# First up projection of a macaron layer: pairs 13 to 21 by seven block products, with the modulation dots moved around them

## The chip, the cores and the metric

The kernel runs on one core of one Trainium2 chip. The metric is the device time of one execution in microseconds (us), median of three runs.

## What is computed

One encoder layer of width 1024 on 512 tokens, in float32: LayerNorm, a half-step SwiGLU FFN, a mixing sub-layer (latent attention beside causal pooling), a second half-step FFN. The change is in the first FFN:

```python
c_act = jax.nn.silu(c)
mod = (c_act @ w_ada[l] + b_ada[l]).reshape(B, N_SUBLAYERS, 3, D)
shift, scale, gate = mod[:, :, 0], mod[:, :, 1], mod[:, :, 2]
h = x * (1.0 + scale[:, 0, None, :]) + shift[:, 0, None, :]
g, u = jnp.split(h @ ffn1_w_in[l], 2, axis=-1)     # 1024 x 5632
y = (jax.nn.silu(g) * u) @ ffn1_w_out[l]           # 2816 x 1024
x = _layernorm(ALPHA * x + 0.5 * gate[:, 0, None, :] * y, post_ln_g[l, 0], post_ln_b[l, 0])
```

## The kernel before

The core's five engines run programs of their own, written out in order by hand, and wait for one another through semaphores. Features lie on the 128 partitions, the 512 tokens along the free dimension. To keep float32 accuracy each operand is split in a high part (rounded to fp32r on ScalarE) and a low part (the rest, on VectorE or GpSimd), and each product is three matmuls: high by high, high by low, low by high.

Weights come in units of 128x1024 (512 KB), that is eight 128x128 blocks, one output tile each. SP loads unit n into a ring of three (`raw`), ScalarE makes w_hi (`act_hi`), VectorE w_lo (`dve_lo`), four slots deep and three units ahead. Pair t of the first up projection (F1) is unit 2t (gate) and 2t+1 (up): 48 matmuls of 512 columns. Then ScalarE applies Silu to the gate bank, VectorE multiplies with the up bank, ScalarE and GpSimd split the result into a_hi, a_lo. There are 22 pairs. The down projection takes three units for each of eight output tiles m (the third with six blocks only), 24 units, and ends each tile by a residual on VectorE. In tile 1 TensorE runs one matmul over x tile 0 (`shift_mean`, which wants ScalarE's rounding of that tile), VectorE copies the result (`shift`), and GpSimd subtracts it from all eight x tiles.

In the second FFN pairs 5 to 21 are already made otherwise (`block_products`). The 2x2 scheme of seven products takes the two halves of the contraction and the two halves of the tokens against combinations of the gate and up blocks: products p1 to p7, each 4 x 3 matmuls of 256 columns, 84 in all. Three of the weight combinations are made by adding DMAs from GpSimd's queue and by VectorE (`weight_sums`), four combinations of h (T) once by VectorE (`combine_h`), the partial results pass through ScalarE's copies (p_copy, u_copy). The SP queue loads for each pair: c, d (raw_d), a3 and ab. The x tiles give up their space for it and are spilled to HBM ahead and reloaded at the start of the down projection.

The 72 modulation columns (`mod`) are dots: VectorE multiplies a tile of w_ada (128x1024, 512 KB, loaded by SP) by c_act and sums it. Sixteen are done at the start. The other 56 come through `ada_ring`, two slots, one after each w_lo of the first up projection (38) and one a unit in the down projection (18). `derive_in`, `derive_gb` and `derive_gate` are small VectorE steps on their results, and `rope_chunk` are VectorE steps for the rotary angles.

## Time and profile before

| what | value |
|---|---|
| median of 3 runs | 938.01 us (937.66 to 938.11) |
| profiled execution, its own time | 938.53 us |
| its span, first to last instruction | 936.7 us |
| TensorE busy | 924.4 us |
| VectorE busy | 600.4 us |
| ScalarE busy | 422.3 us |
| GpSimd busy | 276.1 us |

The span is what the trace covers; the time of the execution is 1.8 us more. An engine that is busy all the time sets the length of the stretch, and an idle one costs nothing unless that engine waits for it. Matmuls overlap, so a matmul's cost is the distance from one start to the next, not its own duration.

### The profile page before, as it was taken

How to read it: one execution, taken by the hardware profiler on the slowest of the kernel's cores; microseconds unless marked ns; L12 is line 12 of the kernel's file. 1: busy time of each engine (PE TensorE's matmuls, PEld its weight loads, DVE VectorE, ACT ScalarE, POOL GpSimd, SP SyncE). 2: the span in 40 equal slices, each digit the busy share in tenths (PEclk: the TensorE clock that was granted, in tenths of full speed). 3: DMA queues.
4: the chain of work that ended last, by engine and by line, in shares of the span. 5: the costliest groups of instructions: out<-in, count | busy, mean ns of one | idle time of the engine just before them, and what ended most of it. 6: DMA issues, size and time to landing. Idle time of an engine off the chain costs nothing.

```text
span 936.7 us, 12697 instructions
## 1 busy us (share of the span) xinstructions
PE 924.4 (99%) x4845; PEld 777.8 (83%) x4845; DVE 600.4 (64%) x875; ACT 422.3 (45%) x673; POOL 276.1 (29%) x239
## 2 busy tenths in 40 slices
PE   8999999999999999999999999999999999999997
PEld 5788888888888888787776677889999999888886
DVE  6956776545454964687775577787777877533334
ACT  6753223332322132483576646655556555322124
POOL 0021111111113522155863655832111110035124
PEclk9999999999999999999999999999999999999999
DMA  9936556556553663314411112286777775623302
GB/s 356 379 117 211 189 192 199 193 180 206 192 175 129 200 240 116 102 68 135 118 63 46 45 54 82 70 255 158 183 190 180 179 193 147 225 79 107 124 18 90
DMA packets 50507, 144.88 MB, mean 155 GB/s; under 512 B 5264, under 2 KB 7440, under 8 KB 50448
## 3 DMA queue, kind: packets, MB, share of 16 engines
q1 hardware_dynamic: 45008, 134.65, 42.3%
q0 software_dynamic: 4896, 8.92, 6.0%
q8 instruction: 38, 0.62, 0.3%
q10 hardware_dynamic: 544, 0.52, 0.2%
q14 instruction: 21, 0.17, 0.1%
HBM read 138.83 MB, written 4.19 MB: 153 GB/s over the span
## 4 chain that ended last, share of the span: by engine, by line
PE 94%; DVE 2%; DMA 2%; ACT 1%; issue 1%; SPq 1%; ACTq 0%; DVEq 0%
PE bank L890 23%; PE bank L892 23%; PE bank L891 23%; PE bank L1001 6%; PE bank L1003 6%; PE bank L1002 6%; PE bank L1307 2%; PE bank L1331 1%; DMA ada_first<-ada_w 1%; PE bank L1318 1%; DMA raw_d<-wunits 1%; PE bank L975 1%; PE bank L1071 1%; PE bank L976 1%; PE bank L969 1%
## 5 line engine op out<-in xcount | busy, mean ns | idle before, releaser
L1434 DVE TENSOR_TENSOR w_lo<-raw,w_hi 128x1024 fp32r<-128x1024 f32 (+1 forms) x117 | 160.7, 1383 | 132.2 <-ACT w_hi L1406 131.8
L890 PE MATMUL bank<-h_hi,w_hi 128*128 128x512 f32 x455 | 178.7, 393 | 0.0
L892 PE MATMUL bank<-h_hi,w_lo 128*128 128x512 f32 x455 | 177.2, 389 | 0.0
L891 PE MATMUL bank<-h_lo,w_hi 128*128 128x512 f32 x455 | 177.2, 389 | 0.0
L1406 ACT ACTIVATE w_hi<-raw 128x1024 fp32r<-128x1024 f32 (+1 forms) x118 | 118.7, 1023 | 117.5 <-PE bank L892 111.5
L890 PE MATMUL bank<-a_hi,w_hi 128*128 128x512 f32 (+1 forms) x338 | 128.0, 379 | 0.0
L891 PE MATMUL bank<-a_lo,w_hi 128*128 128x512 f32 (+1 forms) x338 | 127.7, 378 | 0.0
L892 PE MATMUL bank<-a_hi,w_lo 128*128 128x512 f32 (+1 forms) x338 | 127.7, 378 | 0.0
L2542 POOL TENSOR_TENSOR a_lo<-act_t,a_hi 128x512 fp32r<-128x512 f32 x27 | 37.8, 1398 | 251.2 <-ACT a_hi L1529 251.1
L892 PEld LDWEIGHTS bank<-h_hi,w_lo 128*128 128x128 f32 x455 | 85.4, 188 | 18.1
L890 PEld LDWEIGHTS bank<-h_hi,w_hi 128*128 128x128 f32 x455 | 85.4, 188 | 17.9 <-issue 0.5
L891 PEld LDWEIGHTS bank<-h_lo,w_hi 128*128 128x128 f32 x455 | 85.5, 188 | 17.2
L1892 DVE SCALAR_TENSOR_TENSOR var<-ada_ring,c_act 128x1024 bf16<-128x1024 f32 x56 | 72.5, 1295 | 2.4 <-DMA ada_ring<-ada_w 2.4
L890 PEld LDWEIGHTS bank<-a_hi,w_hi 128*128 128x128 f32 x338 | 63.6, 188 | 11.9
L891 PEld LDWEIGHTS bank<-a_lo,w_hi 128*128 128x128 f32 x338 | 63.6, 188 | 11.8
L892 PEld LDWEIGHTS bank<-a_hi,w_lo 128*128 128x128 f32 x338 | 63.6, 188 | 11.8
L1529 ACT ACTIVATE a_hi<-act_t 128x512 fp32r<-128x512 f32 x40 | 25.3, 632 | 79.3 <-DVE act_t L2050 67.5
L1514 ACT ACTIVATE sq<-x 128x512 f32<-128x512 f32 x20 | 12.6, 632 | 105.7 <-DVE x L2038 96.6
L2563 POOL TENSOR_TENSOR s_sum<-s_sum,x 128x512 f32<-128x512 f32 x17 | 27.5, 1616 | 108.1 <-DVE x L2038 105.8
L1001 PE MATMUL bank<-t_hi,hi 128*128 128x256 f32 x204 | 58.0, 284 | 0.7 <-ACT p_copy L1576 0.6
L1002 PE MATMUL bank<-t_lo,hi 128*128 128x256 f32 x204 | 57.7, 283 | 0.0
L1003 PE MATMUL bank<-t_hi,lo 128*128 128x256 f32 x196 | 55.4, 283 | 0.0
(374 smaller groups left out, 1948.6 us busy)
## 6 DMA issues: line engine op xcount, KB each, us to landing
raw<-wunits SPq DMA_DIRECT2D x110, 512.0 KB, 3.3
ada_ring<-ada_w SPq DMA_DIRECT2D x56, 512.0 KB, 4.3
raw_ab<-wunits SPq DMA_DIRECT2D x18, 512.0 KB, 4.7
ada_first<-ada_w SPq DMA_DIRECT2D x16, 512.0 KB, 11.1
raw<-wunits SPq DMA_DIRECT2D x32, 256.0 KB, 3.7
raw<-wunits POOLq DMA_DIRECT2D x32, 256.0 KB, 4.8
raw<-wunits SPq DMA_DIRECT2D x16, 384.0 KB, 2.9
raw_d<-wunits SPq DMA_DIRECT2D x17, 256.0 KB, 2.8
```

The source lines that it names most:

```text
L890: mm(out, lh, rh, start=first, stop=False)
L891: mm(out, lh, rl, start=False, stop=False)
L892: return mm(out, ll, rh, start=False, stop=last)
L1001: nc.tensor.matmul(out[:, 0:HALF], hi[:, cols], high, start=first and kk == 0, stop=False, skip_group_check=True)
L1002: nc.tensor.matmul(out[:, 0:HALF], hi[:, cols], low, start=False, stop=False, skip_group_check=True)
L1003: done = nc.tensor.matmul(out[:, 0:HALF], lo[:, cols], high, start=False, stop=last and kk == KH - 1, skip_group_check=True)
L1406: nc.scalar.activation(parts(n, 0, width)[0], raw_of(n, width), ACT.Copy)\
L1434: nc.vector.tensor_tensor(lo, raw_of(n, width), hi.bitcast(F32), SUB).then_inc(s_lo, 1)
L1529: fn(a_parts(f, t)[0], act_t[:, t % 2, :], ACT.Copy).then_inc(s_ah[f], 1)
L1892: stt(junk, slot_ap, 1.0, c_act[:], MUL, MUL, accum_out=mod[:, t:t + 1])\
L2542: tt(lo, act_t[:, t % 2, :], hi.bitcast(F32), SUB).then_inc(s_al[f], 1)
L2563: tt(s_sum[:], s_sum[:], x[:, m, :], ADD).then_inc(s_acc[p], 1)
```

## The change

Pairs 13 to 21 of the first up projection are made by the seven block products, with the functions of the second FFN taken for both (`FIRST`, `END`). For it:

- the x tiles are spilled in pair 5 and reloaded at the start of the down projection; the whole h (`h_full1`) is made again by ScalarE in pairs 3 to 10;
- block buffers lie on the weight ring, h_full1 and further ones in the still unused end of a_hi1 and a_lo1, and raw_d, its low parts and the copies lie on c_act and ada_ring. c_act is therefore loaded again and put through Silu again;
- the modulation ring has four slots, the third and fourth in a_hi1 until pair 17 and in the norm buffers and act_t afterwards. 20 dots are in pairs 3 to 10 (three a pair in pairs 5 to 8), none in pairs 11 to 21, and 36 in the down projection: none, 3, 3, 1, 1, 1 in its first six units, then 2, 3, 2 three times, then 2, 2, 2;
- rope chunks start in pair 3, the rope rows of ScalarE are in pair 11; derive_in and derive_gb of the mixing sub-layer come after unit 2 of the down projection.

```diff
-ROPE_FIRST, ROPE_ACT = 4, 16
+ROPE_CHUNKS = {3: (0,), 4: (1,), 5: (2,), 6: (3,), 7: (4,), 8: (5,), 9: (6,), 10: (7, 8)}
...
-T0 = 5
-D2 = F2 + 2 * T0
+FIRST, END = (13, FT + 5), (FT, 2 * FT)
+EDGE = (F1 + 2 * FIRST[0], F2 + 2 * (FIRST[1] - FT))
+SKIP = F1_DOWN - EDGE[0]
+D2 = EDGE[1]
+DOWN_AT = (F1_DOWN, D2)
 STREAM = D2 + DOWN
+DOTS_UP = [0] * EARLY + [1, 1] * 2 + [1, 2] * 4 + [1, 1] * 2
+DOTS_DOWN = [0, 3, 3, 1, 1, 1] + [2, 3, 2] * 3 + [2, 2, 2]
+RING = 4
+ADA_UP = sum(DOTS_UP)
+ADA_STEPS = [list(range(sum(DOTS_DOWN[:i]) + ADA_UP, sum(DOTS_DOWN[:i + 1]) + ADA_UP))
+             for i in range(len(DOTS_DOWN))]
+ADA_UP_STEPS = [list(range(sum(DOTS_UP[:i]), sum(DOTS_UP[:i + 1]))) for i in range(len(DOTS_UP))]
...
+            t_hi1 = sb("t_hi1", [P, 4, KH, HALF], F32R, late)
...
+        ring_a = [sb(f"ring_a{i}", [P, D], F32, late_ctx) for i in range(2)]
+        late_ctx.close()
...
+        h_full1 = sb("h_full1", [P, KD, TOK], F32, late_ctx)
+        raw_13x1 = sb("raw_13x1", [P, 2 * BLOCK], F32, late_ctx)
...
+        raw_d41 = sb("raw_d41", [P, 4, BLOCK], F32, late_ctx)
...
+        def ring_slot(a):
+
+            i = a % RING
+            if i < 2:
+                return ada_ring[:, i, :]
+            return ring_a[i - 2][:] if a < ADA_UP else (ring_norm, ring_act)[i - 2][:]
...
-                if a >= 2:
-                    sp.wait_ge(s_adadone, ADA_FIRST + a - 1)
-                sp.dma_start(ada_ring[:, a % 2, :], ada_w[ADA_FIRST + a]).then_inc(s_ada[a % 2], 16)
+                sp.wait_ge(s_adadone, ADA_FIRST + a - RING + 1)
+                sp.dma_start(ring_slot(a), ada_w[ADA_FIRST + a]).then_inc(s_ada[a % RING], 16)
...
+            def spill_x(f):
+
+                for half in range(2):
+                    k = slice(KH * half, KH * (half + 1))
+                    sp.dma_start(spill[f][k].rearrange("t p n -> p t n"), x[:, k, :]).then_inc(s_spill, 16)
+
+            def reload_x(f, i):
+
+                dst = stream(2 * f + 1)
+                sp.dma_start(dst[:, 2 * i:2 * i + 2, :], spill[f][2 * i:2 * i + 2].rearrange("t p n -> p t n"))\
+                    .then_inc(s_x2[i], 16)
+
+            def load_blocks(f):
+
+                first, end = FIRST[f], END[f]
+                load_c(first)
+                load_d(first)
+                load_ab(first)
+                load_a3(first)
+                load_c(first + 1)
+                load_a3(first + 1)
+                load_ab(first + 1)
+                for t in range(first, end - 1):
+                    if t + 2 < end:
+                        load_c(t + 2)
+                    if t > first:
+                        load_d(t)
+                    if t + 2 < end:
+                        load_a3(t + 2)
+                        load_ab(t + 2)
+                unit(DOWN_AT[f])
+                unit(DOWN_AT[f] + 1)
+                load_d(end - 1)
+                for n in range(DOWN_AT[f] + 2, DOWN_AT[f] + LEAD + 2):
+                    unit(n)
+
+            for i, tiles in enumerate(ADA_UP_STEPS):
+                n = split_next(F1, i)
+                if n is not None and n + RAWS < EDGE[0]:
+                    unit(n + RAWS)
+                for a in tiles:
+                    if a + RING < ADA_UP:
+                        ada(a + RING)
+                if i == EARLY + 4:
+                    sp.wait_ge(*res_done(0))
+                    spill_x(0)
+            load_blocks(0)
+            sp.wait_ge(s_blk, PRODUCT["p3", END[0] - 1])
+            sp.dma_start(c_act[:], c_rows).then_inc(s_c, 16)
+            sp.wait_ge(s_bsum, SUM["gb", END[0] - 1])
+            ada(ADA_UP)
+            reload_x(0, 0)
+            ada(ADA_UP + 1)
+            reload_x(0, 1)
+            ada(ADA_UP + 2)
+            reload_x(0, 2)
+            reload_x(0, 3)
+            sp.wait_ge(s_al[0], FT)
+            ada(ADA_UP + 3)
+            unit(F1_DOWN + LEAD + 2)
+            for i, tiles in enumerate(ADA_STEPS):
+                unit(F1_DOWN + LEAD + 3 + i)
+                for a in tiles:
+                    if a + RING < RING_TILES:
+                        ada(a + RING)
+            for n in range(F1_DOWN + LEAD + 3 + len(ADA_STEPS), MX + RAWS + LEAD):
...
-                    for t in range(EARLY // 2, FT):
+                    for t in range(EARLY // 2, FIRST[0]):
                         up(base, f, t)
                 else:
                     opening(p, base)
                     pe.wait_ge(s_lo, base + OPEN + 1)
                     whole_unit(base + OPEN, bank[up_bank(f, 1) + 1][:], 2)
-                    for t in range(2, T0):
+                    for t in range(2, FIRST[1] - FT):
                         up(base, f, t)
-                    block_products()
+                block_products(f)
...
+                    if f == 0 and 3 <= t < 3 + KD:
+                        k = t - 3
+                        fn(h_full[0][:, k, :], x[:, k, :], ACT.Identity, scale=first_col[:, k, 0:1],
+                           bias=first_col[:, k, 1:2]).then_inc(s_hf[0], 1)
...
+                        if f == 0 and m == 0 and j == 1:
+                            act.wait_ge(s_c, 32)
+                            fn(c_act[:], c_act[:], ACT.Silu).then_inc(s_cact, 1)
...
-                        a = UP - EARLY + DPM * m + j
-                        if f == 0 and a < RING_TILES:
+                        i = DPM * m + j
+                        for a in ADA_STEPS[i] if f == 0 and i < len(ADA_STEPS) else ():
+                            if a == ADA_UP:
+                                dve.wait_ge(s_cact, 3)
                             ada_ring_tile(a)
+                        if f == 0 and i == 2:
+                            dve.wait_ge(s_adadone, ADA_FIRST + 3 * KD)
+                            derive_in(1)
+                            derive_gb(1)
```

The change moves work most at the start of the down projection. SP's queue there before: units of the down projection (the 768 wide one is its unit 2, loaded ahead) and modulation tiles take turns.

```order
L741 DMA raw<-wunits 128x1024 [waits w_lo_done]
L747 DMA ada_ring<-ada_w 128x1024 [waits ada_tiles_done]
L741 DMA raw<-wunits 128x768 [waits w_lo_done]
L747 DMA ada_ring<-ada_w 128x1024 [waits ada_tiles_done]
L741 DMA raw<-wunits 128x1024 [waits w_lo_done]
L747 DMA ada_ring<-ada_w 128x1024 [waits ada_tiles_done]
```

Nothing but weights and modulation tiles stands there. SP's queue at the same place in the changed kernel, from the first load of a down unit on (raw_ab_0 and raw_1_0 are block buffers that hold units 0 and 1; x_transposed_block_products is the semaphore that counts block products). The 768 wide load after ring_act is unit 5.

```order
L854 DMA raw<-wunits 128x768 [waits x_transposed_block_products]
L854 DMA raw<-wunits 128x1024 [waits w_hi_done,x_transposed_block_products] x2
L979 DMA c_act<-c_rows 128x1024 [waits x_transposed_block_products]
L859 DMA ada_ring<-ada_w 128x1024 [waits ada_tiles_done,x_kept_block_sums]
L940 DMA x<-x_spill 128x2x512
L859 DMA ada_ring<-ada_w 128x1024 [waits ada_tiles_done]
L940 DMA x<-x_spill 128x2x512
L859 DMA ring_norm<-ada_w 128x1024 [waits ada_tiles_done]
L940 DMA x<-x_spill 128x2x512 x2
L859 DMA ring_act<-ada_w 128x1024 [waits ada_tiles_done,a_lo_done0]
L854 DMA raw<-wunits 128x768 [waits w_lo_done]
L854 DMA raw<-wunits 128x1024 [waits w_lo_done] x2
```

Between the loads of units 3 and 4 and that of unit 5 there now stand c_act, four modulation tiles and four reloads of x.

ScalarE's queue, before: the rounding of units 3, 4 and 5, then h_hi<-x, which is the rounding of x tile 0 for the mean matmul, then the next units.

```order
L1406 ACTIVATE w_hi<-raw 128x1024 [waits units_used,raw_loaded2]
L1406 ACTIVATE w_hi<-raw 128x1024 [waits units_used,raw_loaded0]
L1406 ACTIVATE w_hi<-raw 128x768 [waits units_used,raw_loaded1]
L1677 ACTIVATE h_hi<-x 128x512 [waits e_done1]
L1406 ACTIVATE w_hi<-raw 128x1024 [waits units_used,raw_loaded2]
L1406 ACTIVATE w_hi<-raw 128x1024 [waits units_used,raw_loaded0]
```

Tile 0 follows directly on unit 5. The same place in the changed kernel:

```order
L1562 ACTIVATE w_hi<-raw 128x1024 [waits x_transposed_block_products,raw_loaded2]
L1562 ACTIVATE w_hi<-raw 128x1024 [waits units_used,raw_loaded0]
L1857 ACTIVATE c_act<-c_act 128x1024 [waits c_loaded]
L1562 ACTIVATE w_hi<-raw 128x768 [waits units_used,raw_loaded1]
L1840 ACTIVATE h_hi<-x 128x512 [waits e_done1]
L1562 ACTIVATE w_hi<-raw 128x1024 [waits units_used,raw_loaded2]
L1562 ACTIVATE w_hi<-raw 128x1024 [waits units_used,raw_loaded0]
```

The order of units 3, 4, 5 and tile 0 is as it was, and the Silu of c_act has come between units 4 and 5.

VectorE's queue, before, from the low part of unit 3 of the down projection to the copy of shift (w_lo is a low part, var,mod a dot, L2038 a residual):

```order
L1434 TENSOR_TENSOR w_lo<-raw,w_hi 128x1024 [waits w_hi_done,derived_columns]
L1892 SCALAR_TENSOR_TENSOR var,mod<-ada_ring,c_act 128x1024 [waits ada_tiles_done,ada_loaded0]
L1434 TENSOR_TENSOR w_lo<-raw,w_hi 128x1024 [waits w_hi_done]
L1892 SCALAR_TENSOR_TENSOR var,mod<-ada_ring,c_act 128x1024 [waits ada_tiles_done,ada_loaded1]
L2038 SCALAR_TENSOR_TENSOR x<-bank,gate,x 128x512 [waits units_used,x_copied]
L1434 TENSOR_TENSOR w_lo<-raw,w_hi 128x768 [waits w_hi_done]
L1892 SCALAR_TENSOR_TENSOR var,mod<-ada_ring,c_act 128x1024 [waits ada_tiles_done,ada_loaded0]
L1434 TENSOR_TENSOR w_lo<-raw,w_hi 128x1024 [waits w_hi_done]
L1892 SCALAR_TENSOR_TENSOR var,mod<-ada_ring,c_act 128x1024 [waits ada_tiles_done,ada_loaded1]
L1434 TENSOR_TENSOR w_lo<-raw,w_hi 128x1024 [waits w_hi_done]
L1892 SCALAR_TENSOR_TENSOR var,mod<-ada_ring,c_act 128x1024 [waits ada_tiles_done,ada_loaded0]
L2035 COPY shift<-bank 128x512 [waits tile0_mean,units_used]
```

Five dots stand ahead of the copy. And in the changed kernel, from the low part of unit 4 to that of unit 6, without the small derive steps that repeat:

```order
L1590 TENSOR_TENSOR w_lo<-raw,w_hi 128x1024 [waits w_hi_done]
L2058 SCALAR_TENSOR_TENSOR var,mod<-ada_ring,c_act 128x1024 [waits ada_tiles_done,ada_loaded0,c_act_ready_root_guess]
L2058 SCALAR_TENSOR_TENSOR var,mod<-ada_ring,c_act 128x1024 [waits ada_tiles_done,ada_loaded1]
L2058 SCALAR_TENSOR_TENSOR var,mod<-ring_norm,c_act 128x1024 [waits ada_tiles_done,ada_first_or_blocks_loaded10]
L2204 SCALAR_TENSOR_TENSOR x<-bank,gate,x 128x512 [waits units_used,x_or_blocks_loaded2]
L1590 TENSOR_TENSOR w_lo<-raw,w_hi 128x768 [waits w_hi_done]
L2058 SCALAR_TENSOR_TENSOR var,mod<-ring_act,c_act 128x1024 [waits ada_tiles_done,ada_first_or_blocks_loaded11]
L2058 SCALAR_TENSOR_TENSOR var,mod<-ada_ring,c_act 128x1024 [waits ada_tiles_done,ada_loaded0]
L2058 SCALAR_TENSOR_TENSOR var,mod<-ada_ring,c_act 128x1024 [waits ada_tiles_done,ada_loaded1]
L2076 TENSOR_TENSOR modb<-mod,cols 128x16 [waits ada_tiles_done]
L1590 TENSOR_TENSOR w_lo<-raw,w_hi 128x1024 [waits w_hi_done]
L2058 SCALAR_TENSOR_TENSOR var,mod<-ring_norm,c_act 128x1024 [waits ada_tiles_done,ada_first_or_blocks_loaded10]
```

Before, one dot follows each low part. Now three dots follow that of unit 4 and three that of unit 5, and the derive steps stand ahead of the low part of unit 6.

## Rows read from the trace of the kernel before

**Rows 1.** The page: busy time of TensorE, and granted clock in tenths.
```profile
PE 924.4 (99%) x4845; PEld 777.8 (83%) x4845; DVE 600.4 (64%) x875; ACT 422.3 (45%) x673; POOL 276.1 (29%) x239
...
PEclk9999999999999999999999999999999999999999
```

**Rows 2.** Windows: us, PE, PEld, DVE, ACT, POOL busy, clock, DMA share, GB/s.
```profile
71.30:158.40 87.10, 87.10 (x386) 72.13 (x385) 60.64 (x90) 25.86 (x33) 10.33 (x8) 1.00 0.61 197
...
730.00:808.00 78.00, 78.00 (x631) 77.04 (x631) 57.99 (x89) 43.57 (x74) 9.55 (x11) 1.00 0.63 170
808.00:818.00 10.00, 10.00 (x49) 8.38 (x48) 3.90 (x5) 3.74 (x5) 0.00 (x0) 1.00 0.97 340
26.00:36.00 10.00, 9.36 (x44) 7.14 (x44) 9.90 (x18) 9.17 (x13) 0.00 (x0) 1.00 1.03 418
```

**Rows 3.** Timeline of PE: start, us, line, operation; first rows of pair 3 and down.
```profile
59.48 0.39 PE L890 MATMUL bank<-h_hi,w_hi 128*128 128x512 f32 x1
...
266.20 0.39 PE L890 MATMUL bank<-a_hi,w_hi 128*128 128x512 f32 x1
```

**Rows 4.** Timeline of PE, second FFN: first matmul of four block pairs.
```profile
637.44 0.35 PE L1001 MATMUL bank<-h_hi,hi_ab 128*128 128x256 f32 x1
...
669.22 0.28 PE L1001 MATMUL bank<-h_hi,hi_ab 128*128 128x256 f32 x1
...
729.70 0.28 PE L1001 MATMUL bank<-h_hi,hi_ab 128*128 128x256 f32 x1
...
739.78 0.28 PE L1001 MATMUL bank<-h_hi,hi_ab 128*128 128x256 f32 x1
```

**Rows 5.** View of tile act_t: durations in ns min/median/max, first and last start.
```profile
L1748 ACT ACTIVATE act_t<-x,first_col x7: 800/815/817, 22.9 to 51.0; 128x512 f32<-128x512 f32 x7
```

**Rows 6.** Timelines of SP, ACT and PE in the third block pair, second FFN.
```profile
643.75 0.33 SPq L834 DMA_DIRECT2D raw_d<-wunits  x1
...
649.97 1.06 ACT L1566 ACTIVATE hi_d<-raw_d 128x1024 fp32r<-128x1024 f32 x1 [1.99 <-DMA raw_d<-wunits]
...
651.74 0.35 PE L1001 MATMUL bank<-t_hi,hi 128*128 128x256 f32 x1 [0.65 <-ACT p_copy L1576]
```

**Rows 7.** Timelines of PE, SP, DVE, ACT, start of the second down projection.
```profile
800.26 0.40 PE L890 MATMUL bank<-a_hi,w_hi 128*128 128x512 f32 x1
...
823.58 0.40 PE L1053 MATMUL bank<-h_hi,ones_t 128*128 128x512 f32 x1
...
807.35 1.92 SPq L863 DMA_DIRECT2D x<-x_spill  x4
809.31 0.52 SPq L741 DMA_DIRECT2D raw<-wunits  x1
...
810.82 0.69 DVE L2205 TENSOR_TENSOR ax_lo<-act_t,ax_hi 128x512 fp32r<-128x512 f32 x1 [0.70 <-ACT ax_hi L1529]
...
817.21 0.85 ACT L1406 ACTIVATE w_hi<-raw 128x768 fp32r<-128x768 f32 x1 [4.52 <-DMA raw<-wunits]
819.21 0.63 ACT L1677 ACTIVATE h_hi<-x 128x512 fp32r<-128x512 f32 x1 [1.15 <-DVE x L2038]
```

**Rows 8.** Timelines of DVE and POOL, first down projection.
```profile
267.48 0.17 DVE L1910 TENSOR_TENSOR modb<-mod,cols 128x16 f32<-128x16 f32 x1
267.69 0.17 DVE L1916 TENSOR_SCALAR scale<-modb 128x8 f32<-128x8 f32 x1
...
282.98 1.22 DVE L1892 SCALAR_TENSOR_TENSOR var<-ada_ring,c_act 128x1024 bf16<-128x1024 f32 x1
...
296.57 0.69 DVE L2035 COPY shift<-bank 128x512 f32<-128x512 f32 x1 [6.25 <-PE bank L892]
...
304.83 2.31 DVE L1892 SCALAR_TENSOR_TENSOR var<-ada_ring,c_act 128x1024 bf16<-128x1024 f32 x1
...
315.99 0.74 DVE L2038 SCALAR_TENSOR_TENSOR x<-bank,gate,x 128x512 f32<-128x512 f32 x1
...
297.34 13.18 POOL L2554 TENSOR_TENSOR x<-x,shift 128x512 f32<-128x512 f32 x8 [28.11 <-DVE shift L2035]
```

More of the change, by code:

```diff
@@ L95, in product_order @@
     out = []
-    for t in range(T0, FT + 1):
-        if t < FT:
-            out += [("p1", t), ("p5", t), ("p6", t)]
-        if t > T0:
-            out.append(("p4", t - 1))
-        if t < FT:
-            out += [("p2", t), ("p7", t)] if t == T0 else [("p7", t), ("p2", t)]
-        if t > T0:
-            out.append(("p3", t - 1))
+    for first, end in zip(FIRST, END):
+        for t in range(first, end + 1):
+            if t < end:
+                out += [("p1", t), ("p5", t), ("p6", t)]
+            if t > first:
+                out.append(("p4", t - 1))
+            if t < end:
+                out += [("p2", t), ("p7", t)] if t == first else [("p7", t), ("p2", t)]
+            if t > first:
+                out.append(("p3", t - 1))
@@ L105, in product_order @@
     return out
 def rounding_order():
-    out = [("T", j) for j in range(4)] + [("ab", T0), ("13", T0), ("2", T0)]
-    for t in range(T0, FT + 1):
-        if t > T0:
-            out.append(("d4", t - 1))
-        if t + 1 < FT:
-            out += [("ab", t + 1), ("2", t + 1), ("13", t + 1)]
+    out = []
+    for f, (first, end) in enumerate(zip(FIRST, END)):
+        out += [("T", 4 * f + j) for j in range(4)] + [("ab", first), ("13", first), ("2", first)]
+        for t in range(first, end + 1):
+            if t > first:
+                out.append(("d4", t - 1))
+            if t + 1 < end:
+                out += [("ab", t + 1), ("2", t + 1), ("13", t + 1)]
@@ L116, in rounding_order @@
     return out
 def rest_order():
-    out = [("T", 0), ("T", 1), ("ab", T0), ("13", T0), ("2", T0), ("T", 2), ("T", 3)]
-    for t in range(T0, FT + 1):
-        if t > T0:
-            out.append(("d4", t - 1))
-        if t + 1 < FT:
-            out += [("ab", t + 1), ("2", t + 1), ("13", t + 1)]
+    out = []
+    for f, (first, end) in enumerate(zip(FIRST, END)):
+        out += [("T", 4 * f), ("T", 4 * f + 1), ("ab", first), ("13", first), ("2", first),
+                ("T", 4 * f + 2), ("T", 4 * f + 3)]
+        for t in range(first, end + 1):
+            if t > first:
+                out.append(("d4", t - 1))
+            if t + 1 < end:
+                out += [("ab", t + 1), ("2", t + 1), ("13", t + 1)]
@@ L147, in silu_order, with combo_key @@
     out = []
-    for t in range(T0, FT + 2):
-        if t - 2 >= T0:
-            out.append(("b", t - 2))
-        if T0 <= t - 1 < FT:
-            out.append(("a", t - 1))
+    for first, end in zip(FIRST, END):
+        for t in range(first, end + 2):
+            if t - 2 >= first:
+                out.append(("b", t - 2))
+            if first <= t - 1 < end:
+                out.append(("a", t - 1))
     return out
 def copy_order():
-    return [(kind, t) for t in range(T0, FT) for kind in ("p1", "u2", "u3")]
+    return [(kind, t) for first, end in zip(FIRST, END) for t in range(first, end) for kind in ("p1", "u2", "u3")]
+def combo_key(f, j):
+    return "T", 4 * f + j
 def counts(order, base):
@@ L327, in build @@
[L327 to L338 removed]
+            blocks = [{}, {}]
@@ L546, in whole_h @@
         def whole_h(p, k):
-            return act_t[:, k % 2, :] if p == 1 else h_full[:, k, :]
+            return act_t[:, k % 2, :] if p == 1 else h_full[1][:, k, :]
         def wg(n):
@@ new lines, in a_low, with block_stage @@
+                dve.wait_ge(s_ah[f], m + 1)
+                dve.wait_ge(s_al[f], m)
+                hi, lo = a_parts(f, m)
+                tt(lo, act_t[:, t % 2, :], hi.bitcast(F32), SUB).then_inc(s_al[f], 1)
+            def block_stage(base, f):
+                first, end = FIRST[f], END[f]
+                weight_sums(first)
+                rest("ab", first)
+                rest("13", first)
+                rest("2", first)
+                product(base, f, local(first) - 1)
+                rest(*combo_key(f, 2))
+                rest(*combo_key(f, 3))
+                for t in range(first, end + 1):
+                    if t >= first + 2:
```

632 lines of the change are left out of this document (332 added, 300 removed).

## The prediction, made before the changed kernel ran

> **What bounds the kernel now.** I read the page first: TensorE is busy 924.4 of 936.7 us, at the upper clock level throughout (the row of granted clock shows 9 in every slice) [rows 1]. So time comes only out of TensorE's own work, or out of the few gaps in it. The windows by stage say the same for the places that the change touches: in the first up projection TensorE is busy 87.10 of 87.10 us, with VectorE at 60.64, and in the block stage of the second FFN 78.00 of 78.00, with VectorE at 57.99 and the DMA engines at 0.63 [rows 2]. The reader is to see that both forms of a pair keep TensorE full once they run, and that neither VectorE nor the DMA engines are near their limit there. The profiled execution took 938.53 us and its span is 936.7; the median of the three runs is 938.01. The sum below is made on the span, and the change is then taken off the median.
>
> **What a pair costs in either form.** From the start of pair 3 to the start of the down projection are 19 pairs: 266.20 - 59.48 = 206.7 us [rows 3], 10.88 us each, or 48 matmuls of 512 columns at 0.2267 us. A block pair in steady state is one step from 729.70 to 739.78, 10.08 us, or 84 matmuls of 256 columns at 0.120 us [rows 4]. Seven eighths of the columns would give 9.52 us; the rest, 13 ns more for each of 84 shorter matmuls, is lost, since 0.2267 is 13 ns over 512 columns at 2.4 GHz and 0.120 is 13 ns over 256.
> The Trainium skill (TensorE: Matmul & The Clock Gate, "Wait — 56ns, not 53.3ns?") gives that fixed part as about 2.5 ns. By it a block pair would take 84 x 109.2 ns = 9.17 us and a plain one 48 x 215.8 ns = 10.36 us, a gain of 1.19 us a pair; the trace has five times the fixed part, and the measurement decides.
> Nine pairs (13 to 21) change form: 9 x (10.88 - 10.08) = **7.2 us** off TensorE. This is the only gain in the change; everything else can only give some of it back.
>
> **What is hidden.** ScalarE makes the eight 128x512 tiles of h_full1 in pairs 3 to 10, about 0.82 us each by the same operation on act_t [rows 5], where it is busy 25.86 of 87.10 us [rows 2]. VectorE gets a third dot in pairs 5 to 8: 7.6 us of each 10.88 now, 8.8 then. The spill of x (2 MB) goes out in pair 5 beside 2.6 MB of loads; the unit loads are three units ahead. I cost these at nothing; were the cover gone, the price would be a wait of a unit, at most 1 or 2 us once.
>
> **The entry into the blocks.** In the second FFN the first three block pairs, 637.44 to 669.22, took 31.78 us where three steady ones take 30.24 [rows 4]: **1.5 us** lost. Most of it is one wait of 0.65 us: the load of raw_d is issued at 643.75, ScalarE rounds it only at 649.97, and TensorE waits at 651.74 for the copy behind it [rows 6]. The first FFN enters by the same order of loads, rounding and sums, so I take the same price. Bounds: 0.3 us if this queue is shorter because the spill went earlier, 3 us if ScalarE's rope rows, now in pair 11, push the rounding of the combinations.
>
> **The start of the down projection.** This is where the gain may go. Today in the first FFN nothing is loaded there but units and one modulation tile a unit. In the new order, once product p3 of pair 21 is done, SP issues c_act (its space was lent out), then three modulation tiles between four reloads of x, a fourth tile, and only then weight unit 5 of the down projection. ScalarE's queue has the rounding of unit 5 ahead of the rounding of x tile 0, and TensorE's queue has the mean matmul, which wants that tile, at the head of unit 4. So TensorE waits at unit 4 for the landing of unit 5.
> The second FFN shows the short form of it. Counted from the start of the down projection at 800.26, the reloads are issued at 7.1 us and ScalarE gets unit 5 at 817.21, that is 9.9 us later, after 2.49 MB; tile 0 is rounded at 819.21 and TensorE runs the mean matmul at 823.58, 23.3 us from the start, with no wait [rows 7]. In the first FFN the issue starts when p3 is done, at about 8.6 us (a_lo of the last pair follows at 810.82), and five transfers of 512 KB are added in front, 2.62 MB. Full-width loads ran at 418 GB/s [rows 2], so they add 6.3 us. Unit 5 lands at 8.6 + 9.9 + 6.3 = 24.8, its rounding takes 0.85 and that of tile 0 0.63: 26.2 us, where TensorE comes at 23.3. Stall: **2.9 us**. Bounds: at the 340 GB/s of 808:818 the added loads take 7.7 us and the stall is 4.3; if the added tiles did not delay the unit it would be nothing.
> The Trainium skill (DMA: Bandwidth & Descriptors, "Specifications") puts the limit of loads from HBM at about 358 GB/s per core; by it the added 2.62 MB take 7.3 us and the stall is 3.9 us. This trace has 418 GB/s over 10 us, so it does not hold here.
>
> **VectorE behind it.** Ahead of its copy of shift VectorE has eight dots instead of five, and they come late. After unit 5 (rounded at 25.7) it makes its low part and three dots, whose tiles land behind units 6 and 7 (4 x 0.524 MB / 418 GB/s = 5.0 us after 24.8, so the last dot ends at 31), then the nine small derive steps at 0.21 us (267.48 to 267.69) [rows 8], 1.9 us, then the low parts of units 6 and 7 and two dots at 1.15 and 1.22: 37.6 us. Only then comes the copy of shift, which today runs at 296.57, 30.4 us from the start. Behind the copy GpSimd subtracts from eight tiles for 13.18 us, and in that stretch VectorE's dots last 2.31 instead of 1.22 us [rows 8]. Today the stretch from the copy to the residual of tile 2 takes 315.99 - 296.57 = 19.4 us with three dots; the new order has six, 3.7 us more: the residual at 60.7. The low part of unit 11 ends some 4.5 us behind it (a wait for ScalarE included), at 65.2, and TensorE wants it at 55.8 + 2.9 (p4 and p3) + 0.2 + 2.9 (stall) = 61.8. That would be 3.4 us. But dots that fall behind the end of GpSimd's work let the low parts beside them run at full speed, which can take back up to 2.1; I take **1.8 us**, with bounds 0 and 4.5 (3.4, and 0.4 for each of tiles 3 to 5, whose seven dots, three low parts, residual and plain low part make about 15.4 us against TensorE's 14.96).
>
> Sum: 7.2 - 1.5 - 2.9 - 1.8 = **1.0 us off**, span 935.7, median 937.0.
>
> **Rivals.**
> (a) The waits of the down projection do not come about, because tiles and units land side by side or VectorE catches up: only the entry is lost, 7.2 - 1.5 = 5.7 us off, 932.3. For it: DMA engines had room to 418 GB/s; unit 5 must land by 21.9 us. Against it: the transfers of one queue landed in order at the end of the second FFN. 0.2.
> (b) Slower: the down projection becomes VectorE's and the DMA queue's. From unit 6 to 17 they carry 27 tiles and 12 units in 60 us, 19.9 MB, 332 GB/s of the 418 seen; if every dot waits for its tile the low parts come late in each of four tiles. It decides once these waits pass 5.7 us; with 4.3 at unit 4 and 4.5 behind it they are 8.8, and the time is 941.1. 0.22.
> (c) The blocks of the first FFN do not reach 10.08 us because something they share with that stage (the lent space in a_hi1, a_lo1 and the ring) holds loads back: at 10.5 us a pair the gain is 3.4 less and with the other terms 940.4; nothing in the trace speaks for it but that the stage is new. 0.08.
>
> **How the numbers follow.** The forecast, waits of 2 to 6 us in the down projection, has 0.5: 934.5 to 938.6. About 0.2% (1.9 us) is what a measurement of this kernel can tell from no change, so of this case 0.18 is faster, 0.32 same. With (a) at 0.2 faster, and of (b) and (c) 0.25 slower and 0.05 same: faster 0.38, same 0.37, slower 0.25. The range from 932.3 of (a) to 940.5, which leaves out the far part of (b).
>
> **What would show it.** Pairs 14 to 21 of the first up projection at 10.08 us, with at most 2 us lost in pairs 13 to 15. A gap of TensorE of 2 to 4 us in front of the mean matmul of tile 0, ended by ScalarE's rounding of tile 0, which itself waited for the load of unit 5. A second gap at unit 10 or 11 ended by VectorE's low part. The copy of shift some 7 us later than today against the start of the down projection. No gap there at all would be (a); many gaps, from tile 2 to tile 5, would be (b). I would be wrong altogether if the block pairs came out at more than 10.3 us.

## The result, and the profile after

The changed kernel takes 941.01 us (median of 5; 940.09 to 942.21) against 937.66 (5; 937.26 to 938.11): ratio 1.0037, 95% interval 1.0024 to 1.005. It is slower by 3.3 us, where 1.0 us off was forecast. The profiled execution took 940.09 us, the fastest of the five; its span is 938.3. With the experiments the kernel before ran again, at medians of 937.64 to 937.81.

Windows of the changed kernel: pairs 3 to 12, the block pairs to the start of the down projection, the down projection (units 0 to 23), and the rest in two parts. Columns as in [rows 2].

```profile
59.26:168.06 108.80, 108.80 (x481) 90.09 (x480) 86.45 (x116) 45.43 (x60) 21.64 (x16) 1.00 0.66 208
168.06:256.79 88.73, 88.38 (x733) 87.98 (x732) 68.01 (x98) 49.56 (x84) 13.93 (x15) 1.00 0.64 161
256.79:388.92 132.13, 124.69 (x555) 101.70 (x554) 99.11 (x145) 37.48 (x49) 32.52 (x20) 1.00 0.74 264
388.92:583.46 194.54, 194.09 (x893) 147.71 (x892) 137.86 (x228) 116.92 (x231) 113.56 (x101) 1.00 0.25 77
583.46:938.30 354.84, 348.29 (x2269) 317.98 (x2267) 224.03 (x300) 166.81 (x265) 98.54 (x87) 0.99 0.52 145
```

The same window of the kernel before, from its first matmul of the down projection to the mixer's first:

```profile
266.20:386.13 119.93, 119.93 (x530) 99.32 (x529) 73.29 (x99) 33.65 (x42) 33.89 (x21) 1.00 0.49 169
```

The reader is to see two things. The blocks paid: from pair 3 to the start of the down projection are 197.5 us where [rows 3] have 206.7. Of these 9.2 us, 2.9 are not a gain, since the products p4 and p3 of the last pair (24 matmuls of 0.120 us) now stand inside the down projection; 6.3 us are. And the down projection gave all of it back: 119.93 + 2.88 = 122.8 us would be a full TensorE, and it took 132.1. **9.3 us of waits** are new, in a stage in which TensorE did not wait before; VectorE's busy time there rose from 73.3 to 99.1 us.

Where they are, from the timeline of PE (start, us, line, operation, idle time before it and what ended it):

```profile
282.08 0.47 PE L1208 MATMUL bank<-h_hi,ones_t 128*128 128x512 f32 x1 [1.81 <-ACT h_hi L1840]
320.95 0.50 PE L1044 MATMUL bank<-a_hi,w_hi 128*128 128x512 f32 x1 [2.54 <-DVE w_lo L1590]
336.65 0.50 PE L1044 MATMUL bank<-a_hi,w_hi 128*128 128x512 f32 x1 [0.42 <-DVE w_lo L1590]
353.24 0.50 PE L1044 MATMUL bank<-a_hi,w_hi 128*128 128x512 f32 x1 [1.32 <-DVE w_lo L1590]
373.83 0.50 PE L1044 MATMUL bank<-a_hi,w_hi 128*128 128x512 f32 x1 [1.24 <-DVE w_lo L1590]
```

The first is the forecast one, in front of the mean matmul at unit 4. The others stand in front of units 11, 14, 17 and 21, each for a low part that VectorE had not made yet. Against the pitch of 0.2267 us they cost 2.0, then 2.8, 0.7, 1.6 and 1.5 us, with 0.4 more at unit 10 and 0.3 in smaller ones.

What VectorE did between the copy of shift and unit 11, and one tile later (timeline of DVE):

```profile
293.08 0.69 DVE L2201 COPY shift<-bank 128x512 f32<-128x512 f32 x1
296.43 0.75 DVE L2204 SCALAR_TENSOR_TENSOR x<-bank,gate,x 128x512 f32<-128x512 f32 x1 [2.65 <-POOL x L2734]
...
301.35 2.31 DVE L2058 SCALAR_TENSOR_TENSOR var<-ada_ring,c_act 128x1024 bf16<-128x1024 f32 x1
...
316.31 0.75 DVE L2204 SCALAR_TENSOR_TENSOR x<-bank,gate,x 128x512 f32<-128x512 f32 x1
319.10 1.79 DVE L1590 TENSOR_TENSOR w_lo<-raw,w_hi 128x768 fp32r<-128x768 f32 x1 [1.38 <-ACT w_hi L1562]
...
331.95 0.75 DVE L2204 SCALAR_TENSOR_TENSOR x<-bank,gate,x 128x512 f32<-128x512 f32 x1
334.75 1.84 DVE L1590 TENSOR_TENSOR w_lo<-raw,w_hi 128x768 fp32r<-128x768 f32 x1 [1.39 <-ACT w_hi L1562]
...
347.42 1.23 DVE L2058 SCALAR_TENSOR_TENSOR var<-ring_act,c_act 128x1024 bf16<-128x1024 f32 x1 [1.10 <-DMA ring_act<-ada_w]
```

From the copy to the end of unit 11's low part are 27.8 us (293.08 to 320.89). TensorE offers 14.96 + 10.88 = 25.8 from the end of tile 1, which is the earliest at which the copy can come, since it stands behind the wait for that tile. From then on VectorE's step from residual to residual is 15.6 us with seven dots (316.31 to 331.95) against TensorE's 14.96. The rows at 319.10 and 334.75 show what the prediction does not name in its list of a tile's instructions (it has a wait for ScalarE once, in front of unit 11): ScalarE rounds a tile's third unit behind its square and its rounding of x, which wait for the residual, so VectorE idles 1.39 us once a tile, and then makes a low part of 0.95 us in 1.8, beside GpSimd's two sums.

The stages outside gave 1.4 us in the profiled execution: pair 3 starts 0.2 earlier, and from the mixer's first matmul to the end are 549.4 us instead of 550.6 (936.7 - 386.13). Of these 1.2, 0.8 is the wait for raw_d of [rows 6] that this execution does not have. Waits of that kind come and go. TensorE waits in block pairs of the second FFN for a copy whose rounding had waited for raw_d in the profiled executions of e1, e3, e5, e7, e10 and e13 too (0.2 to 1.5 us each, not in the pair of [rows 6]), and in none of e4, e6, e9 and e11. So I don't count it to the change; without the 1.2 the span would be 2.8 longer, near the difference of the medians.

### The profile page after: what moved, and what is told of

Read it like the earlier page. It is cut to its first block, busy times and chain, and to the rows that moved or that the text cites. A ratio compares the mean times of both kernels' runs of the same rounds, so it can differ in the third digit from the quotient of the medians.

```text
span 938.3 us, 13680 instructions
## 1 busy us (share of the span) xinstructions
PE 918.8 (98%) x5169; PEld 786.2 (84%) x5169; DVE 655.9 (70%) x964; ACT 455.3 (49%) x740; POOL 281.2 (30%) x248
## 4 chain that ended last, share of the span: by engine, by line
PE 84%; DVE 6%; DMA 4%; issue 4%; ACT 2%; SPq 1%; ACTq 0%; DVEq 0%
PE bank L1044 17%; PE bank L1045 17%; PE bank L1046 17%; PE bank L1155 9%; PE bank L1157 9%; PE bank L1156 9%; DVE var L2058 3%; PE bank L1462 2%; DMA raw<-wunits 1%; PE bank L1486 1%; DMA ada_first<-ada_w 1%; PE bank L1473 1%; DMA ring_act<-ada_w 1%; PE bank L1123 1%; PE bank L1129 1%
## 5 line engine op out<-in xcount | busy, mean ns | idle before, releaser
L1044 PE MATMUL bank<-h_hi,w_hi 128*128 128x512 f32 x311 | 122.6, 394 | 0.0
L1046 PE MATMUL bank<-h_hi,w_lo 128*128 128x512 f32 x311 | 121.2, 390 | 0.0
L1045 PE MATMUL bank<-h_lo,w_hi 128*128 128x512 f32 x311 | 121.1, 389 | 0.0
L1155 PE MATMUL bank<-t_hi,hi 128*128 128x256 f32 x312 | 88.6, 284 | 0.4 <-ACT p_copy L1735 0.3
L1156 PE MATMUL bank<-t_lo,hi 128*128 128x256 f32 x312 | 88.3, 283 | 0.0
L1157 PE MATMUL bank<-t_hi,lo_of_raw 128*128 128x256 f32 x296 | 83.8, 283 | 0.0
L1044 PEld LDWEIGHTS bank<-h_hi,w_hi 128*128 128x128 f32 x311 | 58.4, 188 | 12.5 <-issue 0.5
L1045 PEld LDWEIGHTS bank<-h_lo,w_hi 128*128 128x128 f32 x311 | 58.4, 188 | 11.4
L1155 PEld LDWEIGHTS bank<-t_hi,hi 128*128 128x128 f32 x312 | 59.9, 192 | 1.0 <-DVE lo_13x L2320 0.5
L1156 PEld LDWEIGHTS bank<-t_lo,hi 128*128 128x128 f32 x312 | 59.9, 192 | 0.0
```

Of the source, the lines that this page charges most:

```text
L1044: mm(out, lh, rh, start=first, stop=False)
L1045: mm(out, lh, rl, start=False, stop=False)
L1046: return mm(out, ll, rh, start=False, stop=last)
L1155: nc.tensor.matmul(out[:, 0:HALF], hi[:, cols], high, start=first and kk == 0, stop=False, skip_group_check=True)
L1156: nc.tensor.matmul(out[:, 0:HALF], hi[:, cols], low, start=False, stop=False, skip_group_check=True)
L1157: done = nc.tensor.matmul(out[:, 0:HALF], lo[:, cols], high, start=False, stop=last and kk == KH - 1, skip_group_check=True)
```

## The experiments

The theory (V): VectorE's queue bounds the first down projection, by the number of its dots, by where they stand, and by GpSimd beside them. The rival (D): the queue of transfers does, units and tiles land late. A third possibility was that the waits are separate terms, each worth what it shows.

The table has, for each kernel, the median of its runs with their number, the ratio to the kernel before with its interval, the span of the profiled execution from the first matmul of the down projection to the mixer's first (122.8 is a full TensorE, 119.9 in the kernel before; in e3 and e7 it holds 2.0 us of a wait in front of the mixer's first matmul itself), and the dots that stand before the copy of shift, in units 5 to 7 (beside the subtractions), and behind them.

```
kernel                      median us (n)  ratio   95% interval    down us  dots before/beside/behind
changed                     941.01 (5)     1.0037  1.0024-1.005    132.1    8 / 6 / 22
e2_round_first              939.40 (8)     1.0022  1.0012-1.0032   131.5    8 / 6 / 22
e4_dots_short               933.45 (5)     0.9955  0.9943-0.9967   125.0    8 / 6 / 22, 16 columns each
e5_no_tile_loads            940.48 (8)     1.0029  1.0016-1.0041   130.2    8 / 6 / 22
e6_no_subtraction           933.83 (5)     0.9959  0.9947-0.9971   125.6    8 / 6 / 22
e1_unit5_first              940.17 (12)    1.0026  1.0017-1.0035   132.0    8 / 6 / 22
e3_dots_after_subtraction   937.76 (12)    0.9991  0.9978-1.0005   126.7    6 / 0 / 30
e7_unit5_and_dots           935.84 (11)    0.9975  0.9966-0.9985   124.8    6 / 0 / 30
e13_columns_last            936.34 (11)    0.9982  0.9973-0.9991   122.9    6 / 0 / 30
e10_four_up_only            940.60 (10)    1.0032  1.0020-1.0044   131.8    4 / 6 / 22
e11_up_and_after            933.96 (6)     0.9965  0.9952-0.9977   124.9    4 / 0 / 28
e9_four_dots_up             931.44 (5)     0.9927  0.9916-0.9939   122.9    4 / 0 / 28
e12_before_no_subtraction   937.80 (11)    1.0001  0.9992-1.001    119.9    control on the kernel before
```

**VectorE's time or the transfers?** In e4 the dots keep their loads and waits and lose their length; in e5 they keep their length and lose their loads.

```diff
# e4, in the dot on VectorE
-                stt(junk, slot_ap, 1.0, c_act[:], MUL, MUL, accum_out=mod[:, t:t + 1])
+                w = 16 if t >= ADA_FIRST + ADA_UP else D
+                stt(junk[:, 0:w], slot_ap[:, 0:w], 1.0, c_act[:, 0:w], MUL, MUL, accum_out=mod[:, t:t + 1])
# e5, in the load of a tile on SP; the dot then names the slot's first tile
+                if a >= ADA_UP + RING:
+                    return
```

> The 36 dots of the down projection go over 16 of their 1024 columns (the rest is left out); every tile is still loaded and waited for. Theory V: a dot costs VectorE 0.2 instead of 1.3 us, the waits of TensorE behind unit 5 (7.3 us) go, that in front of the mean matmul (2 us) stays: 933.5 to 934.5 us. Theory D: tiles and units land no earlier, the waits stay within 2 us of what they are: 939 to 941.

> Of the 36 modulation tiles of the down projection only the first four are loaded; the later dots read these again, at full length (what they should sum is left out). 32 transfers of 512 KB go. Theory V: VectorE's load is the same, only its waits for tiles go (1.1 us in front of one dot, 0.2 at another): 939 to 940.5 us. Theory D: the waits behind unit 5 go: 933 to 935.

e4 took 933.45 us, 7.6 less, e5 940.48, 0.5 less and within its spread (938.30, the profiled one, to 942.84). Every wait behind unit 4 is gone in e4, though all tiles are still loaded at the same places. In e5 those at units 14 and 17 are gone (at the latter VectorE had waited 1.10 us for a tile), 1.0 us is left at unit 21 and 2.4 at unit 11:

```profile
319.44 0.62 PE L1046 MATMUL bank<-a_hi,w_hi 128*128 128x512 f32 x1 [2.36 <-DVE w_lo L1592]
```

The waits behind unit 4 come from VectorE's time and not from the transfers, but for the one late tile at unit 17. (The wait that these expectations and the next put at unit 23 is that at 373.83, which is unit 21.)

**What GpSimd has to do with it.** e6 shortens its eight subtractions of shift in the changed kernel; e12 makes the same edit in the kernel before.

```diff
                     for m in range(KD):
-                        tt(x[:, m, :], x[:, m, :], shift[:], SUB).then_inc(s_xs[p], 1)
+                        w = 16 if p == 1 else TOK
+                        tt(x[:, m, 0:w], x[:, m, 0:w], shift[:, 0:w], SUB).then_inc(s_xs[p], 1)
```

> GpSimd's eight subtractions of shift from x in the first FFN go over 16 of 512 columns (the rest is left out). Theory V with contention as the main part: five dots and low parts of 2.3 us run at 1.2, VectorE waits no more 2.65 us for GpSimd at the residual of tile 1, and is some 8 us earlier at unit 11; the wait there (2.7) goes and those at 14 and 17 (2.1) too, since six tens of a us a tile don't use up 8 us; the one at unit 23 may stay: 936 to 937.5 us. Rival (the number of dots alone, contention hidden): 940 to 941.

> A control on the kernel before: its eight subtractions of shift in the first FFN go over 16 of 512 columns (the rest is left out). In the changed kernel the same edit took 7 us. If GpSimd's slowing of VectorE was hidden under slack before the change, it takes nothing here: 937.5 to 938. If the subtractions cost the chip something else (a port, TensorE's reads): 2 us or more off here too.

e6 took 933.83 us, 7.2 less and more than expected; the control took 937.80, no change. The dots beside the subtractions fell back from 2.31 to 1.21 us and VectorE waited 0.52 instead of 2.65 us for GpSimd (timeline of DVE, e6):

```profile
293.25 0.69 DVE L2201 COPY shift<-bank 128x512 f32<-128x512 f32 x1
294.45 0.75 DVE L2204 SCALAR_TENSOR_TENSOR x<-bank,gate,x 128x512 f32<-128x512 f32 x1 [0.52 <-POOL x L2735]
...
301.46 1.21 DVE L2058 SCALAR_TENSOR_TENSOR var<-ada_ring,c_act 128x1024 bf16<-128x1024 f32 x1
...
312.31 1.84 DVE L1590 TENSOR_TENSOR w_lo<-raw,w_hi 128x768 fp32r<-128x768 f32 x1 [1.39 <-ACT w_hi L1562]
```

Unit 11's low part came 6.7 us earlier. The edit takes away two things at once, the slowing and 2.1 us of VectorE's wait for GpSimd at 294.45; e6 alone does not part them. In the kernel before the same slowing is there (2.31 us in [rows 8]) and costs nothing, for its stage has slack. The windows of the down projection, kernel before without the subtractions, and e6:

```profile
266.10:386.03 119.93, 119.93 (x531) 99.29 (x529) 67.71 (x99) 33.83 (x42) 20.67 (x21) 1.00 0.50 169
```

```profile
256.92:382.51 125.59, 123.42 (x555) 102.02 (x554) 93.50 (x145) 37.50 (x49) 19.36 (x20) 1.00 0.76 277
```

The first row is the important one: 5.6 us of VectorE's busy time are gone and TensorE's 119.93 us did not move. The contention is a cost only once the extra dots have used up the slack.

**The wait for ScalarE once a tile.** e2 takes it away by letting ScalarE round a tile's third unit, and VectorE make its low part, before the residual of that tile.

```diff
# ScalarE; VectorE alike, with dve_lo for act_hi and residual for square
+                        early = f == 0 and j == DPM - 1 and m >= 1
+                        if early:
+                            act_hi(act, n)
                         if j == DPM - 1 and m < KD - 1:
                             square(p, m)
...
-                        if n < STREAM:
+                        if n < STREAM and not early:
                             act_hi(act, n)
```

> Theory V (VectorE's queue bounds the first down projection: seven dots a tile, slowed beside GpSimd, and a wait of 1.39 us for ScalarE at each tile's third unit, because ScalarE rounds that unit behind its square and rounding of the x tile): with the rounding and the low part of a tile's third unit ahead of that tile's residual from tile 1 on, the 1.39 us leave VectorE's loop, the step from residual to residual falls from 15.6 to about 14.3 us, the waits at units 14, 17 and 23 (3.5 us) go and that at unit 11 shrinks by a us or more: 936 to 937.5 us against 941.0. Theory D (the queue of transfers: tiles and units land late): nothing changes in what lands when, 940 to 941.

e2 took 939.40 us, 1.6 less: most of the expected 3.5 to 5 us did not come. VectorE's timeline shows why:

```profile
317.38 0.95 DVE L1590 TENSOR_TENSOR w_lo<-raw,w_hi 128x768 fp32r<-128x768 f32 x1
318.25 0.74 DVE L2207 SCALAR_TENSOR_TENSOR x<-bank,gate,x 128x512 f32<-128x512 f32 x1
...
319.57 2.32 DVE L2061 SCALAR_TENSOR_TENSOR var<-ring_norm,c_act 128x1024 bf16<-128x1024 f32 x1
...
322.01 2.12 DVE L2061 SCALAR_TENSOR_TENSOR var<-ring_act,c_act 128x1024 bf16<-128x1024 f32 x1
...
333.93 0.74 DVE L2207 SCALAR_TENSOR_TENSOR x<-bank,gate,x 128x512 f32<-128x512 f32 x1
```

The idle 1.39 us are gone and the low part is back at 0.95, but GpSimd's two sums, which follow each residual, now meet two full dots, 2.32 and 2.12 us instead of 1.23. The step is 15.68 us, as before (15.64). The idle time had kept VectorE out of GpSimd's way. In this execution (940.91 us, above the median) TensorE's waits behind unit 4 were fewer all the same, 2.4 us at unit 12, 0.7 at unit 18 and 1.5 at unit 21, but behind the first of them it ran seven steps of 0.427 us, 1.4 us lost to a lower clock (see the last section).

**Is the forecast stall worth what it shows?** e1 issues unit 5 of the down projection ahead of c_act, the tiles and the reloads of x.

```diff
             load_blocks(0)
+            unit(F1_DOWN + LEAD + 2)
             sp.wait_ge(s_blk, PRODUCT["p3", END[0] - 1])
...
             ada(ADA_UP + 3)
-            unit(F1_DOWN + LEAD + 2)
```

> The load of weight unit 5 of the down projection goes ahead of c_act, the modulation tiles and the reloads of x. The wait of 2 us in front of the mean matmul goes in any case. If the waits of the down projection are separate terms of a sum (as the prediction added them), the time falls by 2 us, to 939. If VectorE's queue sets the end of the stage (its dots still come when their tiles land, a transfer later, and the copy of shift stays near 293 us), TensorE only comes earlier to unit 11 and waits there some 4.5 instead of 2.7 us: 940 to 941.

940.17 us, 0.8 less, within the spread: the wait at unit 4 is gone, and TensorE waits at units 10 and 11 instead (1.1 and 2.7 us against the pitch, 0.4 and 2.8 before).

```profile
313.59 0.50 PE L1044 MATMUL bank<-a_hi,w_hi 128*128 128x512 f32 x1 [0.96 <-DVE w_lo L1590]
...
321.91 0.50 PE L1044 MATMUL bank<-a_hi,w_hi 128*128 128x512 f32 x1 [2.59 <-DVE w_lo L1590]
```

That is 0.6 us more and not 2.0. Of the rest, 1.4 us went into seven steps of 0.427 us behind the second wait, at the lower clock again; the stage as a whole took 131.97 us, as in the changed kernel. The profiled execution (943.70 us) is the slowest of the twelve, and what it lost beyond this lies outside this stage.

**The number of dots or their place?** e3 leaves units 5 to 7 without dots and lets the rest reach to unit 20, with the last derived columns behind them; e7 adds the edit of e1.

```diff
-DOTS_DOWN = [0, 3, 3, 1, 1, 1] + [2, 3, 2] * 3 + [2, 2, 2]
+DOTS_DOWN = [0, 2, 2, 1, 1, 0, 0, 0, 2] + [2, 3, 2] * 4
...
-                    if f == 0 and m == KD - 3:
+                    if f == 0 and m == KD - 2:
```

> The same 36 dots with none in units 5 to 7, beside GpSimd's subtractions, two instead of three in units 1 and 2, and the rest to unit 20; the last derived columns move behind them. Theory V with contention as its main part: six dots leave the stretch in which an instruction of VectorE takes 2.3 us, the residual of tile 2 comes near 307 instead of 316 us, and seven dots a tile (15.6 us against 14.96) don't use up those 9 us until tile 6: the waits behind unit 5 go, that of 2 us stays: 933.5 to 935. Rival (too many dots in all, wherever they stand): 938 to 940.

> Both edits, unit 5 loaded first and no dots beside the subtractions. If with VectorE off the path the wait in front of the mean matmul is worth its 2 us: 931.5 to 933. If VectorE still sets the end: as with the dots alone, 933.5 to 935.

Both came out above their range, 937.76 and 935.84 us. Inside the down projection it went as expected: no wait but that at unit 4, and in e7 none at all. e3's time fits neither theory of its expectation. But 30 dots now stand behind the copy, and VectorE's lag reached the mixer (e3):

```profile
383.81 0.50 PE L1044 MATMUL bank<-h_hi,w_hi 128*128 128x512 f32 x1 [1.80 <-DVE w_lo L1590]
389.10 0.50 PE L1044 MATMUL bank<-h_hi,w_hi 128*128 128x512 f32 x1 [0.24 <-DVE h_lo L2177]
390.88 0.47 PE L1215 MATMUL bank<-hn_hi,ones_d 128*128 128x512 f32 x1 [0.82 <-DVE hn_lo L2184]
```

e13 is e7 with the derived columns moved behind unit 23 (`m == KD - 1` in the last line of the diff) to see whether they are what is late there.

> As the kernel with unit 5 first and no dots beside the subtractions (36 dots down, seven a tile), but its last derived columns (13 small steps, 2.6 us) stand behind unit 23, at the end of the loop, instead of ahead of the low part of the mixer's first unit, where that kernel waited 1.8 us. If VectorE's lag at the mixer is what kept it at 935.8: the wait goes or falls under 0.5 us, VectorE makes the columns in the 1.7 us in which it waits for TensorE's last tile, 933.5 to 934.5. If they delay the residual of the last tile and the root behind it instead: 935.5 to 936.5.

936.34 us: the rival of that expectation. The wait of 1.80 us went, and two of 0.75 and 0.73 us came for the low parts of the last tiles of x; that of 0.82 us for hn_lo stayed as in e3. I read this so that VectorE's sum is what is late, and an order only chooses where it shows. The runs of e3 (933.98 to 941.79) spread more than those of the kernel before.

So fewer dots: e10 only moves four from units 1 and 2 to pairs 3, 4, 9 and 10; e9 does that and leaves units 5 to 7 free and loads unit 5 first; e11 is e9 with unit 5 where the change loads it.

```diff
-DOTS_UP = [0] * EARLY + [1, 1] * 2 + [1, 2] * 4 + [1, 1] * 2
+DOTS_UP = [0] * EARLY + [1, 2] * 8
# e10
+DOTS_DOWN = [0, 1, 1, 1, 1, 1] + [2, 3, 2] * 3 + [2, 2, 2]
# e9, e11 (with the derived columns at m == KD - 2)
+DOTS_DOWN = [0, 1, 1, 1, 1, 0, 0, 0, 2] + [2, 3, 2] * 2 + [2, 2, 2] * 2
```

> The changed kernel with four of its dots moved from units 1 and 2 of the down projection to pairs 3, 4, 9 and 10; unit 5 is loaded where the change has it, and the other dots stand where the change has them. If it is the number of VectorE's instructions ahead of the copy of shift and of unit 11 that counts: two of the four lie behind unit 5's low part, so VectorE is 2.7 us earlier there, each later wait falls by as much, 937 to 938.5 us. If the place beside GpSimd's subtractions is what counts: no change from 941.

> As the one before, and four more of the dots in pairs 3, 4, 9 and 10 of the up projection (three a pair there from 3 to 10), 32 in the down projection. If the waits are gone already, nothing more comes of it: 931.5 to 933, and the pairs stay hidden at 10.88 us. If VectorE was still behind in the last tiles: 1 us or more below the one before. If three dots beside the rope rows are too much for pairs 9 and 10: above it.

> The kernel of 931.4 us (four dots up, none beside the subtractions) with unit 5 loaded where the change has it, behind c_act, the tiles and the reloads. With VectorE off the path the wait in front of the mean matmul stands alone and costs what it shows: 933 to 933.5 us. If VectorE or the transfers give it back later: 931.4.

e10 gained nothing that can be told (940.60 us; its profiled execution, 945.25, is the slowest of ten and lost 5.1 us in the block pairs), and shows that the stretch from the copy to unit 11 stands by itself. VectorE, with fewer dots, now waits for TensorE's tile 1 before the copy, and is late at unit 11 all the same:

```profile
297.01 0.69 DVE L2201 COPY shift<-bank 128x512 f32<-128x512 f32 x1 [2.31 <-PE bank L1046]
...
323.05 1.80 DVE L1590 TENSOR_TENSOR w_lo<-raw,w_hi 128x768 fp32r<-128x768 f32 x1 [1.39 <-ACT w_hi L1562]
```

From 297.01 to 324.85 are 27.8 us, as in the changed kernel. e11 differs from e10 in the place of the dots and of the columns alone and takes 933.96 us: 6.6 us for the place. e9 takes **931.44 us**, 0.9927 of the kernel before, and its stages are full (pairs 3 to 12, and the down projection):

```profile
59.14:168.00 108.86, 108.86 (x482) 90.18 (x481) 91.37 (x124) 45.18 (x60) 21.64 (x16) 1.00 0.71 227
257.16:380.02 122.86, 122.86 (x556) 102.20 (x555) 92.35 (x137) 38.06 (x49) 31.17 (x20) 1.00 0.71 261
```

Three dots a pair from 3 to 10 stay hidden. And between e11 and e9 the wait at unit 4 is worth 2.5 us (2.05 in the stage of the profiled executions), where in the changed kernel the same edit was worth 0.8 (0.2): a wait is worth what it shows only when the next engine is not late as well. e9 beats both kernels with all of the reference computed.

## Why the prediction was wrong

- **7.2 us gross, right.** Pairs 3 to 12 keep 10.88 us (108.80 for ten), and the nine block pairs take 88.73 + 2.88 = 91.6 us, 10.08 each and 0.9 over. e9 turns it into a gain of 6.4 us, which is 7.2 less that entry within 0.1.
- **Hidden at nothing, right** for h_full1, the third dot and the spill: pairs 3 to 12 are full.
- **Entry, 1.5 us: 0.9 here**, within its bounds. Other executions of the same blocks lose more in pair 15, 2.1 us in one wait in e10's profiled one.
- **Start of the down projection, 2.9 us: 2.0.** The mechanism is the forecast one to the instruction. TensorE came at 23.3 us, as worked out; unit 5 was there to be rounded at 23.8 instead of 24.8 (at 280.58, behind c_act, four tiles and four reloads in the queue). The added transfers cost 1 us less than 418 GB/s gives for them.
- **VectorE behind it, 1.8 us: 7.3. This is the step that failed**, by a mis-sized term, and in two parts. First, units 10 and 11: the working gave 3.4 us, and I took off half for dots that "fall behind the end of GpSimd's work". The trace has 23.2 us from the copy to the residual of tile 2, where the working had 23.1, and 3.2 us of waits; the working was right and the discount was not. GpSimd's eight subtractions ended at 307.0, but its two sums followed at once until 311.5, and VectorE's dot at 308.24 and low part at 310.28 still took 2.12 and 2.29 us: five of VectorE's instructions were slowed, as before the change, both full-width low parts among them. Second, tiles 3 to 5, for which I allowed 0.4 each and only in the bound: there it was 3.8 us, at units 14, 17 and 21. The step of 15.4 us came near the measured 15.64, though the instructions that the working names make only 13.4 us at full speed (seven dots of 1.22, low parts of 1.23, 1.23 and 0.95, 0.75 and 0.74); the trace fills the rest with the wait of 1.39 us for ScalarE and the low part at 1.8 instead of 0.95. Such a step is 0.7 us over TensorE's, not 0.4: that is unit 14. At unit 17 came a tile that landed 1.10 us late, and at unit 21 the thirteen small steps of 2.6 us ahead of its low part, which the text named for gb(1) and forgot for the end. Once VectorE is late with no slack, each of them is a wait of TensorE.
- **Rival (b)** had the mechanism and the time (941.1, with 8.8 us of waits; 9.3 measured), at 0.22. It named VectorE and the DMA queue; e4 and e5 split these, and it is VectorE.
- The range ended 0.5 us below the result. Its bound of 4.5 us for this term had no place for a late tile or for the small steps at the end, so it was no bound. (In rival (c), nine pairs at 10.5 us instead of 10.08 give back 3.8 us and not 3.4.)

Not settled: why the executions of e3, e10 and e13 spread over 3 to 8 us. The profiled ones show two places of it. The block pairs of the first FFN lose from 0 (e6) to 5.1 us (e10), those of the second from 0 (e9) to 2.5 (e3), there mostly in waits behind a late load of raw_d; and TensorE's clock falls behind some waits, some 1.4 us each time. Why it comes so in one execution and not in another stays open, and so does how much of the 3.3 us of the medians is the clock: the profiled execution of the changed kernel has no such fall, and its four slower ones were not profiled.

## What to carry to other kernels

When work moves into a stage whose second engine is at 61% (73.3 of 119.9 us), sum that engine's loop between two points where it must meet the first, waits for a third engine and slowed instructions included, and not its busy time: the loop here had 0.7 us a tile too much at a busy share of 75% of the stage. A slowing that costs nothing before a change (e12) can be its largest cost after it (e6), so look at what stands beside the slowed stretch before filling it. And remove waits from the back: the one that is seen first was worth 0.8 us while a later one stood behind it, 2.5 when none did.
